# A state space stage threaded between its weight slots, with the turn table doubled on VectorE

## The reference

```python
h = rms_norm(x, norm_g)
proj = h @ w_in;  u, z = proj[..., :1024], proj[..., 1024:]
dt = exp(log_dt);  mag = exp(lr * dt)
ab = mag * cos(li * dt), mag * sin(li * dt)          # complex decay per group and state
f = (ab - 1) / (lr + i li);  in = f * (u @ b)        # 64 groups of 16 channels, 64 states
s = associative_scan(ab, in)                         # along the 256 positions
y = Re(s @ c) + d_skip * u;  y = gelu(y)
y = y * sigmoid(y @ w_glu + b_glu)
x = x + (y * silu(z)) @ w_out
```

## Time and profile before

| what | us |
|---|---|
| median of 3 runs | 1456.99 (1455.03 to 1459.4) |
| the profiled execution, whole time | 1455.84 |
| its span | 1454.0 |
| PE busy | 1283.2 (88%) |
| VectorE busy | 964.9 (66%) |
| ACT busy | 627.1 (43%) |
| GpSimd busy | 181.4 (12%) |
| chain that ended last | PE 77%, DVE 14%, ACT 3%, POOL 3%, issue 2% |

### The profile page before, as it was taken

One profiled execution on the slowest core, in us unless ns is written; L12 is line 12 of the kernel. 1 busy time (PEld: TensorE's weight loads), 2 busy tenths in 40 slices (PEclk: granted clock), 3 DMA queues, 4 the chain that ended last, 5 costly groups with the idle time before them and its releaser, 6 DMA issues.

```text
span 1454.0 us, 18974 instructions
## 1 busy us (share of the span) xinstructions
PE 1283.2 (88%) x7276; PEld 1074.3 (74%) x7276; DVE 964.9 (66%) x1467; ACT 627.1 (43%) x951; POOL 181.4 (12%) x185
## 2 busy tenths in 40 slices
PE   4946379899888999999979999799999989799997
PEld 2435267678777788877779998587788877699986
DVE  4569966585655799768655665447798586565553
ACT  2123134455545455445444444344655453444442
POOL 1995500120010001010010000200010010100000
PEclk9968599999989999999989999899999999899999
DMA  6612045455254544525546656554445435455662
GB/s 214 191 58 63 18 150 171 118 180 166 73 166 127 174 159 146 174 78 183 159 134 187 187 175 198 147 165 160 145 135 170 131 125 168 135 181 183 190 191 88
DMA packets 71852, 216.81 MB, mean 149 GB/s; under 512 B 16545, under 2 KB 20017, under 8 KB 71505
## 3 DMA queue, kind: packets, MB, share of 16 engines
q1 hardware_dynamic: 68112, 205.39, 45.2%
q0 software_dynamic: 2480, 9.06, 2.1%
q10 hardware_dynamic: 1168, 1.14, 0.2%
HBM read 210.05 MB, written 3.15 MB: 147 GB/s over the span
## 4 chain that ended last, share of the span: by engine, by line
PE 77%; DVE 14%; ACT 3%; POOL 3%; issue 2%; DMA 1%; ACTq 0%; SPq 0%; POOLq 0%; DVEq 0%
PE acc L580 16%; PE acc L581 16%; PE acc L582 16%; PE acc L549 6%; PE acc L551 6%; PE acc L550 6%; PE acc L512 4%; POOL stat L1913 2%; PE turned L623 2%; DVE b_mats L1294 2%; PE mixed L769 1%; DVE scan_work L1294 1%; DVE weights_lo L1261 1%; PE mixed L779 1%; DVE junk L1294 1%
## 5 line engine op out<-in xcount | busy, mean ns | idle before, releaser
L1261 DVE TENSOR_TENSOR weights_lo<-weights_raw,weights_hi 128x1024 fp32r<-128x1024 f32 (+2 forms) x364 | 444.0, 1232 | 253.5 <-ACT weights_hi L945 252.2
L945 ACT ACTIVATE weights_hi<-weights_raw 128x1024 fp32r<-128x1024 f32 (+2 forms) x364 | 377.8, 1049 | 313.8 <-PE acc L582 198.9
L580 PE MATMUL acc<-weights_hi,act_F_hi 128*128 128x512 f32 (+1 forms) x864 | 354.8, 411 | 6.2 <-DVE weights_lo L1261 3.3
L581 PE MATMUL acc<-weights_lo,act_F_hi 128*128 128x512 f32 (+1 forms) x864 | 344.8, 399 | 0.0
L582 PE MATMUL acc<-weights_hi,act_F_lo 128*128 128x512 f32 (+1 forms) x864 | 343.9, 398 | 0.0
L549 PE MATMUL acc<-act_F_hi,weights_hi 128*128 128x256 f32 x704 | 199.5, 283 | 0.0
L550 PE MATMUL acc<-act_F_hi,weights_lo 128*128 128x256 f32 x704 | 199.0, 283 | 0.0
L551 PE MATMUL acc<-act_F_lo,weights_hi 128*128 128x256 f32 x704 | 198.9, 283 | 0.0
L580 PEld LDWEIGHTS acc<-weights_hi,act_F_hi 128*128 128x128 f32 x864 | 166.3, 192 | 43.3 <-DVE weights_lo L1261 4.4
L582 PEld LDWEIGHTS acc<-weights_hi,act_F_lo 128*128 128x128 f32 x864 | 166.2, 192 | 38.1
L581 PEld LDWEIGHTS acc<-weights_lo,act_F_hi 128*128 128x128 f32 x864 | 166.6, 193 | 35.0
(11 more groups left out here) (278 smaller groups left out, 1502.6 us busy)
## 6 DMA issues: line engine op xcount, KB each, us to landing
weights_raw<-stream_dram SPq DMA_DIRECT2D x364, 512.0 KB, 4.1
gains<-rows_dram POOLq DMA_DIRECT2D x14, 512.0 KB, 4.1
weights_raw<-stream_dram SPq DMA_DIRECT2D x8, 416.0 KB, 3.2
weights_raw<-stream_dram SPq DMA_DIRECT2D x4, 384.0 KB, 4.8
x_T<-x_in_dram SPq DMA_DIRECT2D x1, 1024.0 KB, 4.9
ssm_bc<-ssm_bc_dram POOLq DMA_DIRECT2D x1, 1024.0 KB, 5.1
u_scratch<-u_T ACTq DMA_DIRECT2D x4, 256.0 KB, 4.7
u_sub<-u_scratch SPq DMA_DIRECT2D x16, 64.0 KB, 2.7
```

The source lines that it names most:

```text
L580: pe.matmul(o, xh, wh, start=first and kk == 0, stop=False)
L581: pe.matmul(o, xh, wl, start=False, stop=False)
L945: act.activation(w_hi[:, s % R, 0:n], raw[:, s % R, 0:n], ACT.Copy).then_inc(hi_made, 1)
L1261: dve.tensor_tensor(w_lo[:, s % R, 0:n], raw[:, s % R, 0:n], w_hi[:, s % R, 0:n].bitcast(F32), ALU.subtract).then_inc(lo_made, 1)
```

## The change

1. **Order.** PE's list is rewritten: eight whole slots, then the quarters with the other eight slots put between their steps. `own_steps` of a quarter is no longer cut in four pieces between transposes.
2. **The norm.** PE turns x itself, which comes in four parts; the gain of the norm is applied by ACT when it copies the turned tiles (a column from `column_rows`), and the root is applied by ACT to u and inside the tanh of z. VectorE no longer runs `apply_norm` for this layer.
3. **c_mats.** Four products on VectorE, stored as four matrices, without the two combining operations; PE's `states_part` sums them and does 64 matmuls a quarter where there were 32.
4. **b and c by pair.** ACT copies b and c once into an order in which 16 channels of a pair lie next to each other (`ssm_by_pair`); `b_mats`, `c_mats` and `c_pairs` read that. The factor f goes into the powers.
5. **The skip and the gelu.** PE adds d to the diagonal of the taps (`d_pattern`, two small matmuls a quarter). The gelu is done on the block layout straight from PSUM: ACT squares, VectorE one sum (two operations), ACT tanh, VectorE one product (four operations of 128 elements a lane) into `y_sub`, which then goes to DRAM and back.
6. **The turn table** is doubled by VectorE (`all_turns`), after `b_mats(1)`. GpSimd sets memory, copies decays, and takes the roots.
7. **Scratch.** u and y are laid out in DRAM so that one transfer does what four did.
8. **Rope tables** of the second block move behind the y gate, to VectorE `rope_angles`/`rope_tables` and one Sin on ACT.

The core of the diff:

```diff
-            turn("hn", DT, tiles_of(hT), lambda t, k: (rows_normed, t + 1), True)
-            run(12)
+            turn("hn", DT, tiles_of(xT), lambda t, k: (x_in4[k // 2], 16), True)
+            run(4)
...
-            taps_and_turned_b(0, lambda n: None)
-            state_terms(0)
-            for qd in range(PARTS):
-                done = 0
-                if qd + 1 < PARTS:
-                    done = 3 if qd > 0 else 0
-                    taps_and_turned_b(qd + 1, lambda n: own_steps(qd, n) if qd > 0 else None)
-                    state_terms(qd + 1)
-                for j in range(done, JB):
-                    own_steps(qd, j)
-                states_part(qd)
-            pe.wait_ge(y_copied, 2 * PARTS)
+            taps(0)
+            run(1)
+            turned_taps_and_b(0)
+            state_terms(0)
+            run(1)
+            taps(1)
+            run(1)
+            turned_taps_and_b(1)
+            own_steps(0)
+            states_part(0)
+            state_terms(1)
+            run(3)
+            taps(2)
+            run(1)
+            turned_taps_and_b(2)
+            state_terms(2)
+            own_steps(1)
+            states_part(1)
+            run(1)
+            taps(3)
+            turned_taps_and_b(3)
+            state_terms(3)
+            own_steps(2)
+            states_part(2)
+            own_steps(3)
+            states_part(3)
+            pe.wait_ge(gelu_made, PARTS)
...
+            def own_steps(qd):
+                pe.wait_ge(toeplitz_in, 16 * SUB * (qd + 1))
+                pe.wait_ge(u_groups_copied, qd + 1)
+                if qd > 0:
+                    pe.wait_ge(gelu_made, qd)
...
+            def all_turns():
+
+                dve.wait_ge(turns_half, 1)
+                dve.wait_ge(b_mats_made, 2)
+                step = (par[:, 14, :], par[:, 15, :])
+                n = 1
+                while n < NSUB:
...
+                    tt(w0, a_r, b_r, ALU.mult).then_inc(dve_steps, count())
+                    tt(w1, a_i, b_i, ALU.mult).then_inc(dve_steps, count())
+                    tt(w2, a_r, b_i, ALU.mult).then_inc(dve_steps, count())
+                    tt(w3, a_i, b_r, ALU.mult).then_inc(dve_steps, count())
+                    if 2 * n < NSUB:
...
+                        tt(c2, step[0], step[0], ALU.mult).then_inc(dve_steps, count())
+                        tt(s2, step[1], step[1], ALU.mult).then_inc(dve_steps, count())
+                        tt(cs, step[0], step[1], ALU.mult).then_inc(dve_steps, count())
+                    dve.wait_ge(dve_steps, count.n)
+                    tt(turn[:, 0, :, n:2 * n], w0, w1, ALU.subtract).then_inc(dve_steps, count())
+                    i = tt(turn[:, 1, :, n:2 * n], w2, w3, ALU.add)
...
             def b_mats(qd):
 
                 if qd > 0:
                     dve.wait_ge(mixed, mix_at[f"ssm{qd - 1}.bt3"][0] + 1)
...
             b_mats(0)
+            c_mats(0)
             b_mats(1)
+            all_turns()
+            scan_states(0)
+            c_mats(1)
+            gelu_sum(0)
+            evac("ssm_in.2")
+            b_mats(2)
+            gelu_product(0)
+            scan_states(1)
+            c_mats(2)
+            gelu_sum(1)
+            b_mats(3)
+            gelu_product(1)
+            scan_states(2)
+            c_mats(3)
+            gelu_sum(2)
+            evac("ssm_in.3")
+            gelu_product(2)
+            scan_states(3)
...
+            ssm_steps = {8: lambda: (load_u(0), load_u(1)), 12: lambda: load_u(2), 13: lambda: toeplitz(0), 15: lambda: toeplitz(1),
+                         16: lambda: load_u(3), 18: lambda: y_to_rows(0), 19: lambda: toeplitz(2),
+                         20: lambda: (y_to_rows(1), toeplitz(3), y_to_rows(2), y_to_rows(3))}
```

More of the change, by code:

```diff
@@ L158, in build @@
     NS = len(slots)
-    u_scr = nc.dram_tensor("u_scratch", [SEQ, D], F32, kind="Internal").ap()
-    y_scr = nc.dram_tensor("y_scratch", [SEQ, D], F32, kind="Internal").ap()
+    for c in table.values():
+        c["par"] = 0 if WHOLE // 2 <= c["first"] < WHOLE else c["index"] % 2
+    u_scr = nc.dram_tensor("u_scratch", [PARTS * JB, SEQ, GB * GROUP], F32, kind="Internal").ap()
+    y_scr = nc.dram_tensor("y_scratch", [PARTS * JB, SEQ, GB * GROUP], F32, kind="Internal").ap()
     ctx = ExitStack()
@@ L1069, in _, with gained @@
-            run(16)
+            def gained(k):
+                n = turn_at[f"hn.{k // 2}"][0]
+                act.wait_ge(turned, n + 1)
+                for kk in range(2):
+                    x = act.activation(f0[:, k + kk, :], turned_bank[n % 2][:, kk * SEQ:(kk + 1) * SEQ], ACT.Copy,
+                                       scale=cols_F[:, k + kk:k + kk + 1])
+                x.then_inc(turned_hi, 1)
+            act.wait_ge(cols_copied, 1)
+            gained(0)
+            gained(2)
+            act.wait_ge(angles, 1)
@@ new lines, in _ @@
+            act.activation(par[:, 3:5, :].rearrange("p a q -> p (a q)"), ang_w[:, 2 * Q:4 * Q], ACT.Sin).then_inc(sines, 1)
+            gained(4)
+            for k in range(DT // 2):
+                act.wait_ge(x_in4[k], 16)
+            a = stats_of("hn", 6)
+            for t in range(TT):
+                squares(xT[:, t, :], a[:, t:t + 1], norm_sums, t + 1)
+            gained(6)
+            act.wait_ge(ssm_mats_in, 16)
+            for n in range(4):
+                x = act.activation(bcq[:, n, :, :], bc[:, n, :, :].rearrange("p c q -> p q c"), ACT.Copy, scale=-1.0 if n == 3 else 1.0)
+                if n % 2:
+                    x.then_inc(pairs_ordered, 1)
@@ L1138, in _ @@
[L1138 to L1141 removed]
+            order_u(0)
+            run(4)
+            taps(0)
+            turned_taps_and_b(0)
+            pair_c(1)
+            group_u(0)
+            order_u(1)
+            taps(1)
+            turned_taps_and_b(1)
+            pair_c(2)
+            gelu_square(0)
+            group_u(1)
+            order_u(2)
+            gelu_tanh(0)
@@ new lines, in _ @@
+            evac("ssm_in.2")
+            taps(2)
+            turned_taps_and_b(2)
+            pair_c(3)
+            group_u(2)
+            order_u(3)
+            gelu_square(1)
+            gelu_tanh(1)
+            evac("ssm_in.3")
+            pos = WHOLE
+            taps(3)
+            turned_taps_and_b(3)
+            group_u(3)
+            gelu_square(2)
+            gelu_tanh(2)
+            act.wait_ge(y_ready, 2 * (PARTS - 1))
+            splits(WHOLE + R - 1)
+            gelu_square(3)
@@ L1595, in _ @@
+            splits(WHOLE + 2)
+            gelu_sum(3)
+            gelu_product(3)
+            splits(WHOLE + R - 1)
+            turn_lo("y", f_hi, f_lo, DT, 0.5)
+            for k in range(PARTS):
+                dve.wait_ge(y_landed[k], 16 * TT)
+            a = stats_of("hn", 6)
             for t in range(TT):
-                tt(yT[:, t, :], yT[:, t, :], zT[:, t, :], ALU.mult).then_inc(dve_steps, count())
+                stt(yT[:, t, :], zT[:, t, :], a[:, 2 + t:3 + t], yT[:, t, :]).then_inc(dve_steps, count())
```

577 lines of the change are left out of this document (285 added, 292 removed).

## The result

The changed kernel takes **1421.16 us** (median of 4 runs, 1418.51 to 1426.16) where the kernel before took 1457.38 in the same session (1455.03 to 1459.4). The ratio is 0.9756, with a 95% interval of 0.9725 to 0.9787: 36 us faster. The forecast was 1418, with 1404 to 1440 as its range.

The account below looks back on a forecast made before the run. VectorE was taken to bound the state space stage, with PE waiting. The first split slot moves from 204.07 to 164.6 us, so 1455.84 - 39.5 + 2 = 1418 us, range 1404 to 1440.

Parts of the forecast that it names:

- What bounds it, and the form of the chain: State space stage bound by VectorE; the question is when PE can start the first split slot.
- The price of the products: VectorE's products in b_mats cost 1.14 us each instead of 1.94; six operations take 6.9 us.
- Rival (a): Products of b_mats stay at 1.94 us, +9.6 us on the path, time 1428; chance 0.13.
- The turn table: 50 VectorE operations on the path after b_mats(1), 12.6 us in sum, ending at 66.3 us.
- By itself this move is a loss: Moving the turn table to VectorE loses; on GpSimd it was ready at 70 us, first read at 107.34.
- The start: ACT's first Exp needs ssm_dt alone; first whole slot at 9.9 us, eight slots end at 38.9.
- `states_part`: PE's step doubles from the old row: 5.0 us in full clock, 7.2 after a gap.
- The clock: PE work after a long gap runs in the lower clock, charged 2.2 us extra.
- Rival (b): PE's clock stays down from 72 to 142 us, +25 us, time 1443; chance 0.11 in part or whole.
- the 0.8 named as a sign: A PE clock under 0.8 from 70 to 140 us would show the forecast wrong.
- From the eighth slot to the first split slot: Stretch of PE's chain through the quarters, from 38.9 us to the first split slot at 164.6 us.
- Costs behind it, +2: Beyond the stage: two ACT table loads and missed handoffs add 2 us; VectorE's rope tables add nothing.

Follow-up runs that it names:

- experiment 3: The changed kernel, but the products of b_mats read b as loaded, 16 channels 32 values apart; ratio 0.9826 to the kernel before.
- experiment 2: The changed kernel, but GpSimd doubles the turn table again, as in the kernel before; 1413.37 us, ratio 0.97.
- experiment 1: The changed kernel with VectorE doubling the turn table ahead of b_mats(1); 1410.4 us, ratio 0.9677.
- experiment 8: The changed kernel with turn table ahead of b_mats(1), b_mats(2) and b_mats(3) ahead of gelu sums, last scan ahead of gelu_sum(2); 1401.26 us.
- experiment 7: The changed kernel with unused transposes filling five PE waits, in counts of 56, 42, 28, 24 and 24; 1413.11 us, ratio 0.9704.
- experiment 4: The changed kernel with the last scan ahead of gelu_sum(2) on VectorE; 1422.16 us, ratio 0.9753.
- experiment 5: The changed kernel with all sixteen whole slots first again, ahead of quarter 0, VectorE's cheaper operations kept; 1439.68 us, ratio 0.9882.
- experiment 9: The kernel of experiment 8 plus unused transposes ahead of own_steps(3) (18) and the turning of y (15); 1400.53 us, ratio 0.9615.
- short fill: The changed kernel with unused transposes in five PE waits, in counts of 36, 26, 18, 15 and 15; 1418.61 us, ratio 0.9733.

## Why the prediction was right, and where its steps were off

The forecast of 1418 was 3 us under the measured 1421.16. Point by point:

- **What bounds it, and the form of the chain:** right. The waits of PE before `states_part(0)`, `taps(3)` and `states_part(3)` were named with their cause, and VectorE's idle time before `b_mats(1)` too. The wait of 3.66 us before `own_steps(3)`, for `gelu_product(2)`, is in the sum but was not charged in clock.
- **The price of the products** (1.14 a piece against 1.94): right, rows at a spacing of 1.14 to 1.25 us, and experiment 3 shows the cause. Rival (a) is out. The ACT rows that it leaned on carried less than was read from them: dense, the same four copies still take 1.04 us, so of the 0.37 us of one only 0.11 was the stride.
- **The turn table:** 12.6 us forecast, 11.5 measured. "By itself this move is a loss" was right and is now measured: 7.8 us against GpSimd (experiment 2), 10.8 against its own best place (experiment 1).
- **The start:** off. The first whole slot was put at 9.9 us, it came at 12.26. What was off is that the Exp gates it. The Exp ran at 4.43 us; the slot stood behind the third pair of transposes of x, and those waited for their transfers (1.24, 2.03 and 1.40 us). The eight slots ended at 42.85 instead of 38.9. This beginning differs between executions of the same code: the first eight matmuls took 6.19 us here and 4.59 in the profile of experiment 8, later ones 3.6 to 3.7.
- **`states_part`:** off. Doubling the old row gave 5.0 us in full clock and 7.2 behind a wait; measured are 5.98 twice, 7.76 and 7.38, together 2.7 us more. One matmul of it takes 46.7 ns where it took 38.8 (2.48 / 64); why is not shown.
- **The clock:** the mechanism was right (2.2 us for work behind a gap), and its size about so. Three such charges came to 6.4 us. Against the long fill of experiment 7 the same three cost 1.8 us (`states_part(0)`), 2.6 (from `taps(3)` to its block terms) and 1.4 (`states_part(3)`), together 5.8. Left out were 1.5 us in the block terms and own steps around 110 to 115 us (clock 0.70; block terms 3.17 instead of 2.06 us with only a handoff of 1.52 us before them) and 0.8 in the turning of y, which makes 8.1 in all. Rival (b) did not occur: the clock did not stay down through the middle but was 0.99 from 85 to 110 us and 1.00 from 115 to 125; its mean from 70 to 140 us is 0.85, above the 0.8 named as a sign.
- **From the eighth slot to the first split slot:** 125.7 forecast, 128.8 measured. With the start, the first split slot is 7.1 us later than forecast (171.68 against 164.6).
- **"Costs behind it, +2":** wrong in sign. From the first split slot to the end the profile shows 1249.9 us before and 1247.5 after. Two table loads and the rope tables cost nothing to be seen. Nor can the -2.4 be put down to the change: from the row of the next norm on GpSimd to the end, the profiles of the changed kernel and of experiments 1, 2, 4, 5, 7, 8 and 9, all with the same program there, give 1190.6 to 1194.7 us, and the kernel before gives 1193.1. This scatter of 4 us is also why experiment 4's 1.9 us could not be seen in its time.

So 1418 was near because two errors of opposite sign largely cancelled, +7.1 up to the first split slot (4.0 at the start, 3.1 behind it) and -4.4 after it. That closeness is luck: the chain was the right one, with its largest waits in their places, but without the second error the forecast would have been 7 us off, still inside its range.

The rows of that last point: GpSimd in the kernel before, the changed one and experiment 8.

```profile
260.93 0.57 POOL L1913 TENSOR_TENSOR stat<-stat,minus_half 128x1 f32<-128x1 f32 x1
```

```profile
228.31 0.57 POOL L2083 TENSOR_TENSOR stat<-stat,minus_half 128x1 f32<-128x1 f32 x1
```

```profile
206.01 0.57 POOL L2083 TENSOR_TENSOR stat<-stat,minus_half 128x1 f32<-128x1 f32 x1
```

With the spans of 1454.0, 1419.2 and 1400.7 us these leave 1193.1, 1190.9 and 1194.7.

Still open: how the 17 us that slots-first keeps divide between the cheaper reads, the early Exp, and GpSimd's silence. Experiment 3 gives 10 for the reads in the changed kernel's order, but experiments in another order need not add up. Nor was the fall of the clock at 110 us tried by itself; it was there with the short fill (block terms 3.26 us) and in experiment 2 (3.60), where no wait stood before `states_part(0)`, and gone with the long fill and in experiments 1 and 8 (2.06). What decides it stays open.

## What to carry to other kernels

When a list of one engine is written by hand, look in its timeline for a long wait followed by work that did not need what was waited for; here four blocks, moved with nothing else changed, gave 20 us on top of the change's 36. Price a moved piece of work by its place as much as by its engine: the same table on VectorE took 7.8 us more than on the slower GpSimd at one place in the list, and 3 us less at another. And when PE waits in a stage of small matmuls, charge the work behind the wait in the lower clock too (here 1.4 to 2.6 us behind the charged waits, though one wait of 3.66 us cost anything from 0 to 2); filling the wait is a quick test of that, removing it is the cure.

## What the runs showed of the hardware that was not expected

- Useless transposes in PE's waits made the kernel 8.0 us faster (1413.11 against 1421.16). With 2.78 us of wait left before it `states_part(0)` took 7.62 us, with 0.56 left 5.98. With 1.37 left `states_part(3)` took 5.98.
- Behind the same wait of 3.66 us, and with the same PE work ahead of it, `own_steps(3)` took 2.43 us in the changed kernel, 3.48 in experiment 2 and 4.47 in experiments 1 and 4. Block terms behind the same handoff of 1.52 us took between 2.06 and 3.60 us. In quarter 0 they took 2.06 in the changed kernel and 2.94 in experiment 4, which up to there are the same program: where the lower clock falls can differ between executions, and 1 to 3 us of a stage with it.
- At the start, the first eight matmuls of the whole slots took 6.19 us against 3.6 to 3.7 later, in a stretch whose row says clock 1.00. One matmul of 512 columns took up to 1.06 us there and 0.59 later. So in the first microseconds the durations are a better guide than that column.
- A tensor operation of 1024 elements on VectorE takes 1.95 us with one operand strided by 128 bytes and 1.22 dense, and ACT's four copies of the same data into `c_pairs` went from 1.48 to 1.04 us.
- Beside GpSimd's doubling VectorE's 1024-element operations took 1.22 to 2.18 us (1.22 alone), and a combining one 3.49 beside the heavier products of the kernel before; a 32-element operation of GpSimd's took 1.27 us instead of 0.32. Both engines lose, and the loss was larger beside the larger operations.
